# One range instruction for each run of neighbouring semaphore numbers at the end of a stage, in a ten-stage decoder step

## The reference

```python
h = rmsnorm(x, nrm[0])
xm, v, ig, fg, og, qn, kvc, kvs, kvw, gn, ga, gb = split_in(h @ p['w_in'])
hm, C, n, m, mconv_new = mlstm_mixer(xm, v, ig, fg, og, mconv, C0, n0, m0, p)
on, new_rows, new_win = nsa_mixer(qn, kvc, kvs, kvw, gn, qpos, past, win_buf, wb, rel_table, p)
merged = jax.nn.sigmoid(ga) * (hm @ p['w_up_m']) + jax.nn.sigmoid(gb) * (on @ p['w_up_n'])
x = x + rmsnorm(merged @ p['w_out'], nrm[1])
...
x = x + rmsnorm(ox @ p['x_wo'], nrm[3])
h = rmsnorm(x, nrm[4])
u, fconv_new = causal_dwconv(h @ p['f_wu'], fconv, p['f_conv_w'], p['f_conv_b'])
x = x + rmsnorm((jax.nn.gelu(u) * (h @ p['f_wg'])) @ p['f_wd'], nrm[5])
```

## Time and profile before

| what | value |
|---|---|
| time, median of 3 runs | 2566.96 us (2557.03 to 2568.64) |
| time of the profiled execution | 2567.4 us |
| its span, first to last instruction | 2565.6 us |
| mean granted clock of TensorE in it | 0.944 of full speed |
| busy: TensorE / VectorE / ScalarE / GpSimd | 2302.4 / 1088.7 / 692.6 / 416.0 us |

### The profile page before, as it was taken

How to read it: one execution, slowest core, us unless ns; L and a number is a source line. 1 busy time by engine, 2 the same in 40 slices (tenths; PEclk the granted TensorE clock), 3 DMA queues, 4 the chain that set the end, 5 groups by cost and what they waited for, 6 DMA issues and landing times. The chain is left out here.

```text
span 2565.6 us, 41143 instructions
## 1 busy us (share of the span) xinstructions
PE 2302.4 (90%) x15977; PEld 2084.9 (81%) x15977; DVE 1088.7 (42%) x2461; ACT 692.6 (27%) x1391; POOL 416.0 (16%) x374
## 2 busy tenths in 40 slices
PE   8999675877898888999899979898999999999995
PEld 7799654764555558999798957698999999999995
DVE  2212255124666663132227104418655555553335
ACT  3210153103565552011134002425211111121122
POOL 0000011230322302212011100011222121222220
PEclk9999887787998998999899989899999999999997
DMA  3211202787443423111311043512111111111312
GB/s 136 96 49 48 17 1 90 265 288 282 163 140 103 153 74 111 50 50 38 117 46 34 23 142 136 213 34 101 50 50 42 50 43 49 44 40 45 111 40 76
DMA packets 114348, 233.22 MB, mean 91 GB/s; under 512 B 23442, under 2 KB 76339, under 8 KB 110723
## 3 DMA queue, kind: packets, MB, share of 16 engines
q1 hardware_dynamic: 85034, 177.94, 21.0%
q0 software_dynamic: 10368, 28.33, 3.4%
q10 hardware_dynamic: 18754, 24.35, 2.8%
HBM read 207.28 MB, written 27.47 MB: 92 GB/s over the span
## 5 line engine op out<-in xcount | busy, mean ns | idle before, releaser
L88 PE MATMUL psum<-x_half_high,ff_half 128*128 128x352 f32 x3240 | 791.4, 324 | 14.1 <-DVE h_again_low L69 9.2
L88 PEld LDWEIGHTS psum<-x_half_high,ff_half 128*128 128x128 f32 x3240 | 568.1, 189 | 15.4 <-DVE ff_half L69 9.4
L88 PE MATMUL psum<-h_again_low,ff_half 128*128 128x352 f32 x1176 | 378.7, 322 | 0.0
L69 POOL TENSOR_TENSOR ff_half<-ring,ff_half 128x1024 fp32r<-128x1024 f32 (+2 forms) x85 | 177.1, 2084 | 761.5 <-ACT ff_half L3048 761.5
L88 PEld LDWEIGHTS psum<-h_again_low,ff_half 128*128 128x128 f32 x1176 | 222.4, 189 | 0.0
L88 PE MATMUL psum<-merged_high,oq_half 128*128 128x352 f32 x768 | 189.6, 327 | 12.9 <-DVE oq_half L69 12.8
L3048 ACT ACTIVATE ff_half<-ring 128x1024 fp32r<-128x1024 f32 (+2 forms) x88 | 78.0, 888 | 433.5 <-PE psum L88 407.5
L88 PE MATMUL psum<-mid_low,ff_half 128*128 128x352 f32 x516 | 166.9, 324 | 0.0
L88 PEld LDWEIGHTS psum<-merged_high,oq_half 128*128 128x128 f32 x768 | 136.2, 191 | 13.5 <-DVE oq_half L69 13.0
L88 PE MATMUL psum<-h_high,in_half 128*128 128x352 f32 x528 | 126.1, 321 | 0.0
L88 PE MATMUL psum<-x_half_high,mg_w_high 128*128 128x352 f32 x384 | 123.9, 323 | 1.2 <-ACT gated L2179 1.2
(11 more groups left out here) (551 smaller groups left out, 4225.2 us busy)
## 6 DMA issues: line engine op xcount, KB each, us to landing
na_kv<-in_pool SPq DMA_DIRECT2D x128, 128.0 KB, 3.5
na_kv<-in_pool POOLq DMA_DIRECT2D x128, 128.0 KB, 4.0
sab_kv<-in_pool SPq DMA_DIRECT2D x96, 128.0 KB, 4.4
mg_w<-in_w_merge SPq DMA_DIRECT2D x16, 768.0 KB, 4.4
sab_kv<-in_pool POOLq DMA_DIRECT2D x88, 128.0 KB, 4.8
ring<-in_f_wu SPq DMA_DIRECT2D x22, 512.0 KB, 3.7
ring<-in_f_wg SPq DMA_DIRECT2D x22, 512.0 KB, 3.7
sab_kv<-in_pool ACTq DMA_DIRECT2D x72, 128.0 KB, 4.6
```

What stands on the lines that cost most here:

```text
L69: return engine.tensor_tensor(low, x, high.bitcast(F32), ALU.subtract)
L88: ins = nc.tensor.matmul(out, w[a], x[b], start=first and n == 0, stop=last and n == 2)
```

## The change

At the end of a stage the numbers of its semaphores are sorted and cut into runs of neighbours. Each run is cleared by one instruction that names a first and a last number. The barriers before and after are as they were, and the same semaphores are cleared.

```diff
         with ExitStack() as ctx:
             yield ctx, sem
-        for s in used:
-            nc.sync.sem_clear(s)
+        numbers = sorted(s.num for s in used)
+        first = [n for n in numbers if n - 1 not in numbers]
+        last = [n for n in numbers if n + 1 not in numbers]
+        for a, b in zip(first, last):
+            nc.sync.sem_clear(range(a, b + 1))
         nc.all_engine_barrier(sem_only=True)
```

## The result

The change is 0.66% faster: 2548.9 us median of 7 runs (2544.78 to 2557.19) beside 2567.07 of the kernel before (2557.03 to 2568.8, 7 runs), ratio 0.9934 with a 95% interval of 0.992 to 0.9948. The forecast was 2550 us. Run twice more on other occasions, the same kernel gave 0.9933 (0.9916 to 0.9951) and 0.9939 (0.9922 to 0.9955).

The account below looks back on a forecast made before the run. TensorE bounds the kernel as a whole, but SyncE's clears lie bare at ten stage boundaries. 18.6 us less 0.3, 0.4 and 0.8 gave 17.1 us off the median 2566.96, so 2550 us, range 2542 to 2559.

Parts of the forecast that it names:

- The clears lie bare, with a 57 ns step, and nothing covers them: Ten stage ends: SyncE's 309 single clears start 57 ns apart while no engine computes, 18.6 us from first to last starts.
- The next stage's first loads move along: Behind the second barrier: a stage's first transfers are issued earlier too, so waiting for them takes none of the gain back.
- The sum, 18.6 - 0.3 - 0.4 - 0.8 = 17.1 us: Ten stage ends: 18.6 us of clears, less 0.3 for clears kept, 0.4 for TensorE reporting last, 0.8 for pauses.
- 0.3 were expected: Stage ends: 15 clears are left, so 5 steps of 57 ns, 0.3 us, stay.
- The 0.4 for a later TensorE: Second barrier of seven single-clear stages: TensorE reports last by up to 0.1 us each; half taken, 0.4 us.
- The 0.8 for pauses: Bursts of `front`, `nsa`, `xk`: pauses total 1.4 us; between all gone and all back, the middle, 0.8 us, is lost.
- The prediction's condition: SyncE's pauses: if they belong to positions in its instruction stream, removing 294 instructions moves them.
- One range clear costs what a single one does: Stage ends: a range clear takes a 57 ns step whatever its range; a clear of 50 numbers lasts 25 to 50 ns.
- a duration in proportion to the numbers: Range clears at stage ends: lasting in proportion to their numbers would show the prediction wrong.
- the rival: Range clears work number by number, 28 ns each: 8.7 us stay, 2558 us; chance 0.12, shared with a recording cost.
- The clock could go either way: TensorE's clock behind boundaries: 10 us more or less gain, 2540 or 2560 us; chance 0.07 better, 0.08 worse.
- more than 10 us' worth: TensorE's clock: a difference above 10 us' worth at the same work between both kernels would show the prediction wrong.

## Why the prediction was right

*The clears lie bare, with a 57 ns step, and nothing covers them.* Shown from both sides: twice the clears costs 18.5 us at the boundaries, and the same clears moved inside the next stage save 12.5 us between two kernels that both lack the second barrier.

*The next stage's first loads move along.* Shown by `na_raw`, issued 5.44 us ahead of TensorE's start in the change and 5.65 before, and by single clears without the second barrier, which stay within 0.24% of before.

*The sum, 18.6 - 0.3 - 0.4 - 0.8 = 17.1 us.* The boundaries lost 17.6 us, and term by term it reads 18.55 - 0.44 - 0.52 - 0. The clears that are left take 0.44 us from first to last start, where 0.3 were expected. The 0.4 for a later TensorE has another cause than the one given: the clear itself lasts longer. At 94 to 113 ns that of `front`, `mlstm` and `sab` keeps SyncE level with TensorE, both reports in the rows at 299.9. From the last clear's start to the release the ten boundaries took 1.9 us before and 2.4 after; that the difference is near the forecast's 0.4 is luck. (The stages with a single clear are six, not seven, which changes that term by 0.05 us.) The 0.8 for pauses was too cautious: none is left at a boundary. The prediction's condition, that they belong to positions in SyncE's stream, was right, and removing 294 instructions did move them. That all of them now fall where they cost nothing is luck of the count: 1.4 of the 17.6 us hang on it, and a program with a few instructions more or less could have one back on the path.

*One range clear costs what a single one does.* Wrong in the mechanism, and too small to matter. The prediction gave a clear of 50 numbers 25 to 50 ns, and named a duration in proportion to the numbers as a sign of being wrong. It lasts 109 to 113 ns, some 28 ns and 1.6 ns for each number, so that sign has come in part. 309 numbers make 0.5 us, part of which lies beside TensorE's report. So the rival was right about the kind of work and wrong about its price. Its 28 ns, and with it the estimate of 29 ns from the Trainium skill (Runtime: NRT & Kernel Launch, the preamble and postamble breakdown), isn't what this instruction does; 29 ns for each number would have made the clear of 50 last 1.4 us, and it lasts 0.11.

*The clock could go either way.* Not shown in either direction. Its mean over the span was higher in all three traces of the change (0.947, 0.949, 0.949) than in both of before (0.944, 0.942). That alone is no gain, as the time taken away held no work, some of it at the low level (0.50 at the end of `ff`). What costs is TensorE's work at the low level: by the clock's and the matmuls' records 155 and 172 us of it before, and 165, 153 and 149 us in the change. The means differ by 8 us, of which half, 4 us, would be time, and the traces of one kernel differ by about 16 us. So the prediction's sign of being wrong, more than 10 us' worth, isn't met, and a help of 4 us is neither shown nor excluded. The medians fell by 18.2, 17.6 and 16.6 us in the three comparisons, and the boundaries by 17.6, which leaves little for it. No long stretch of `ff` fell to the low level.

The no-second-barrier kernel is faster than the change, 0.9911 beside 0.9939 on one chip, and is the version to keep. It relies on two neighbouring stages never sharing a semaphore number.

## What to carry to other kernels

At a barrier, count what stands on the sequencer that everybody waits for, and read its price from start to start, not from the duration of a row: 17 and 28 ns instructions both cost 57 ns here. Busy time doesn't show such work at all. Bookkeeping between two stages is free where its engine waits anyway, and costs its full length ahead of the next stage's first load, barrier or not. For a gain of 0.7% compare the changed stretches of two traces; the spans of the three traces of the change scatter by 8 us, half of the gain. And compare an experiment with the runs that differ from it in one thing only: a kernel that moved the clears and also dropped a barrier looked as fast as the change for two reasons at once.

## What the runs showed of the hardware

- A range clear on SyncE lasts 31 ns for two numbers and 106 to 113 for 50, and the next instruction starts 30 ns after its end; instructions of 17 or 28 ns start 57 ns apart.
- Single clears in a row are 57 ns apart on SyncE, about 65 on GpSimd and ScalarE, 83 on VectorE and 117 on TensorE. Side by side on five engines, SyncE's steps stay at 58 ns (nine steps in 0.53 us).
- SyncE's stream has pauses of 0.34 to 0.45 us at a fixed count: behind its 79th record and behind every 128th after it, in all fourteen traces, with one slip of 18 records late in the program. Three lay bare within the clears of before; none did in the change.
- The length of `sab`, at a DMA share near 0.8, varied between 152.5 and 159.1 us in three executions of one kernel.
